# Hybrid decoder trunk: order of weighting, turning and scoring within a pair of attention heads

## What is computed

```
sc  = einsum('bqgrd,bgnd->bgrqn', qb, k_cmp)
o_c = einsum('bgrqn,bgnd->bqgrd', masked_softmax(sc, ...), v_cmp)
o_s = einsum('bgrqkl,bgqkld->bqgrd', masked_softmax(ss, m_s), vs)
o_w = einsum('bgrqk,bgkd->bqgrd', masked_softmax(sw, m_w), vw)
return gb[..., 0:1] * o_c + gb[..., 1:2] * o_s + gb[..., 2:3] * o_w
```

## Time and profile before

| what | value |
|---|---|
| median of 3 runs | 939.73 us (939.57 to 939.92) |
| the profiled execution's own time | 938.7 us |
| its span | 936.9 us |
| TensorE busy | 893.0 us, 95% |
| VectorE busy | 588.0 us, 63% |
| ScalarE busy | 523.8 us, 56% |
| the attention loop, rounds 1 to 7 | from about 636 to 686 us of the span |
| chain that ended last | TensorE 74%, ScalarE 12%, VectorE 10% |

### The profile page before, as it was taken

One profiled execution on the slowest core, in us unless ns is written; L12 is line 12 of the kernel. 1 busy time (PEld: TensorE's weight loads), 2 busy tenths in 40 slices (PEclk: granted clock), 3 DMA queues, 4 the chain that ended last, 5 costly groups with the idle time before them and its releaser, 6 DMA issues.

```text
span 936.9 us, 14028 instructions
## 1 busy us (share of the span) xinstructions
PE 893.0 (95%) x5289; PEld 758.1 (81%) x5289; DVE 588.0 (63%) x980; ACT 523.8 (56%) x931; POOL 23.9 (3%) x46
## 2 busy tenths in 40 slices
PE   6989999999999999999999999998889999999998
PEld 5989988787888878888888789886567888888876
DVE  5876985767666475555544676777757555554465
ACT  6645666767776474444543559356856544443352
POOL 6000000000000000000000000000000000000000
PEclk9999999999999999999999999999999999999999
DMA  9941211111114557777555555420034565654652
GB/s 342 337 139 43 91 46 46 46 46 46 46 54 171 186 161 247 236 226 224 187 189 176 195 178 177 136 91 1 2 115 154 184 188 186 191 193 158 195 185 93
DMA packets 105898, 138.28 MB, mean 148 GB/s; under 512 B 4585, under 2 KB 76786, under 8 KB 105842
## 3 DMA queue, kind: packets, MB, share of 16 engines
q1 hardware_dynamic: 103650, 130.15, 43.1%
q0 software_dynamic: 2160, 7.36, 2.0%
q10 hardware_dynamic: 32, 0.01, 0.0%
HBM read 136.45 MB, written 1.05 MB: 147 GB/s over the span
## 4 chain that ended last, share of the span: by engine, by line
PE 74%; ACT 12%; DVE 10%; issue 3%; DMA 1%; SPq 0%; ACTq 0%; DVEq 0%
PE ps L504 16%; PE ps L506 16%; PE ps L505 16%; PE ps L483 5%; DVE w_lo L1588 4%; ACT w_hi L1114 4%; PE ps L488 3%; PE ps L490 3%; PE ps L489 3%; PE ps L735 2%; DVE gdn L1655 2%; PE ps L715 2%; PE ps L1000 1%; ACT qkvT L1522 1%; ACT scr L1363 1%
## 5 line engine op out<-in xcount | busy, mean ns | idle before, releaser
L1588 DVE TENSOR_TENSOR w_lo<-w_raw,w_hi 128x2048 fp32r<-128x2048 f32 (+2 forms) x100 | 220.7, 2207 | 195.8 <-ACT w_hi L1114 195.7
L1114 ACT ACTIVATE w_hi<-w_raw 128x2048 fp32r<-128x2048 f32 (+2 forms) x100 | 184.5, 1845 | 181.8 <-PE ps L506 143.2
L504 PE MATMUL ps<-w_hi,x_hi 128*128 128x512 f32 x480 | 193.1, 402 | 5.3 <-DVE x_lo L1621 1.9
L506 PE MATMUL ps<-w_hi,x_lo 128*128 128x512 f32 x480 | 187.6, 391 | 0.0
L505 PE MATMUL ps<-w_lo,x_hi 128*128 128x512 f32 x480 | 187.2, 390 | 0.0
L504 PEld LDWEIGHTS ps<-w_hi,x_hi 128*128 128x128 f32 x480 | 90.2, 188 | 25.9 <-issue 4.5
L506 PEld LDWEIGHTS ps<-w_hi,x_lo 128*128 128x128 f32 x480 | 90.1, 188 | 19.5
L505 PEld LDWEIGHTS ps<-w_lo,x_hi 128*128 128x128 f32 x480 | 90.4, 188 | 16.7
L488 PE MATMUL ps<-x_hi,w_hi 128*128 128x256 f32 x320 | 91.4, 286 | 1.1 <-DVE w_lo L1588 0.8
L489 PE MATMUL ps<-x_lo,w_hi 128*128 128x256 f32 x320 | 90.6, 283 | 0.0
L490 PE MATMUL ps<-x_hi,w_lo 128*128 128x256 f32 x320 | 90.6, 283 | 0.0
(11 more groups left out here) (311 smaller groups left out, 1453.4 us busy)
## 6 DMA issues: line engine op xcount, KB each, us to landing
w_raw<-in_ffn_w_in SPq DMA_DIRECT2D x88, 512.0 KB, 4.6
w_raw<-in_ffn_w_out SPq DMA_DIRECT2D x40, 512.0 KB, 4.1
w_raw<-in_gdn_w_in SPq DMA_DIRECT2D x28, 512.0 KB, 4.7
gdn<-in_gdn_w_in SPq DMA_DIRECT2D x20, 512.0 KB, 7.6
w_raw<-in_gdn_w_out SPq DMA_DIRECT2D x16, 512.0 KB, 4.3
w_raw<-in_ple_w_gate SPq DMA_DIRECT2D x16, 512.0 KB, 4.6
w_raw<-in_kv_w SPq DMA_DIRECT2D x12, 512.0 KB, 4.3
qkvT<-in_cmp_w POOLq DMA_DIRECT2D x8, 512.0 KB, 4.9
```

The lines of the kernel that those rows point to most:

```text
L504: mm(o, hi, w_h, start=first and kk == 0, stop=False, skip_group_check=True)
L506: return mm(o, lo, w_h, start=False, stop=end and kk == n - 1, skip_group_check=True)
L1114: A(whi[:, place(stage, q), c0:c0 + n], ring_raw(u) if stage == "qkv" else raw[:, q, 0:n], ACT.Copy).then_inc(S["hi_done"], 1)
L1588: V.tensor_tensor(wlo[:, s, c0:c0 + n], ring_raw(u) if stage == "qkv" else raw[:, q, 0:n], whi[:, s, c0:c0 + n], ALU.subtract).then_inc(S[ ...
```

## The change

TensorE does the turns of both heads of a pair one behind the other, and the second scores of the next pair behind both. VectorE does the weights of both heads one behind the other, and all four maxima of the next pair behind both. ScalarE's order is untouched.

```diff
@@ TensorE, round p @@
                     scores(p + 1, 0)
                 turned(p, 0)
+                turned(p, 1)
                 if p < 7:
                     scores(p + 1, 1)
-                turned(p, 1)
                 if p == 1:
                     pe.wait_ge(S["q_sb"], 4)
                     cmp_scores(1, 1)
@@ VectorE, round p @@
                 weights(p, 0)
+                weights(p, 1)
                 if p < 7:
                     maxima(p + 1, 0, 0)
                     maxima(p + 1, 1, 0)
-                weights(p, 1)
-                if p < 7:
                     maxima(p + 1, 0, 1)
                     maxima(p + 1, 1, 1)
                 if p == 1:
```

## The result

The changed kernel takes 940.88 us (median of 20 runs, 939.72 to 943.18) against 939.83 us (20 runs, 938.25 to 940.65), a ratio of 1.0015 (95% interval 1.0008 to 1.0021). It is 1.05 us slower by the medians, 1.4 by the ratio. Measured again beside the experiments it was 941.97 us against 938.96, ratio 1.0027 (1.0016 to 1.0039). The prediction was 940.8, no difference beyond 0.2%.

What follows compares the result with a forecast made beforehand. No engine is full; a loop of handovers bounds the stage. Terms 0.55 - 0.02 + 0.55 - 0.07 + 0.06 = +1.07 us on the profiled 938.7 give 939.8, 940.8 on the median's scale; range 939.5 to 942.6.

Steps and rivals of the forecast that it cites:

- The 0.69 of idling goes, and the wait for the maxima takes its place: Ordinary rounds: TensorE's 0.69 idling before the output product is replaced by ScalarE's wait for second maxima; 6.79 against 6.82 us.
- The ordinary round: Rounds 2, 4, 5 and 6: 6.79 us each; -0.02 for round 2, about -0.07 for 4 to 6 together.
- (c): Condition for head 1's turns: the bank of head 0's first turn must be copied; latest of three, at 4.53 us.
- Round 1: Head 1's turns wait for weights, delaying second and compressed scores: +0.55 us taken, from values +0.45 and +0.62.
- The upper of my two values: Round 1 with turns taking 0.93 us: +0.62 us, against +0.45 if the turns need only 0.76.
- The sum: All rounds' terms added: 0.55 - 0.02 + 0.55 - 0.07 + 0.06 = +1.07 us.
- Round 3: Second compressed weights stand behind second maxima, delaying pair 3's weights: +0.55 us taken, from +0.44 (turns in 0.76) and +0.61.
- Round 7: No scores there; head 1's weights follow head 0's and start at 3.40 to 3.42 instead of 3.36: +0.06 us.
- Idling that simply goes: Next exponentials follow ScalarE's copies without waiting for second maxima: 0.75 us a round faster, 937.0 us; chance 0.07.
- VectorE's ring at more than its rows: VectorE's instructions in a round don't overlap: 7.11 us (942.1) or 7.83 us (944.9) where 6.79 was forecast; chance 0.13.
- Absorption behind the loop: The wait for the copy costs less, or something behind the stage takes up the loss: 939.7 to 940.0 us; chance 0.10.
- The granted clock should stay at 1.00: TensorE's clock in the profile after: 1.00, as before with TensorE idle for over a fifth of the first stretch.

Runs made afterwards that it cites:

- short_first: The changed kernel with ScalarE doing the short exponentials of both heads first, then the long ones of both; 942.84 us (ratio 1.0035).
- tail_in_gap: The changed kernel with VectorE's low half and weight quarter moved ahead of the second maxima, from round 3 on; 941.55 us (ratio 1.0021).
- after_heads: The changed kernel with the second scores made head by head, all of head 0 then all of head 1; 942.93 us (ratio 1.0036).
- before_heads: The kernel before, with the second scores made head by head; 943.55 us (ratio 1.0042).
- scale_in_gap: The changed kernel with four of five VectorE steps of the second compressed weights moved ahead of round 2's second maxima; 940.65 us (ratio 1.0016).
- short_first_before: The kernel before, with only ScalarE's exponentials reordered: short ones of both heads first, then long ones; 942.47 us (ratio 1.0035).
- dve_only: The kernel before with only VectorE's order changed: weights of both heads, then all maxima; 939.69 us (ratio 1.0001).
- round3_new: The kernel before, with the new order in round 3 alone, on both engines; 938.83 us (ratio 0.9996).
- pe_only: The kernel before with only TensorE's order changed: turns of both heads, then second scores; 944.31 us (ratio 1.0052).
- round1_old: The changed kernel, with round 1 alone in the order of before on both engines; 941.07 us (ratio 1.0018).
- short_first_gap: The changed kernel with short exponentials first, VectorE's low half, quarter and four compressed steps ahead of second maxima, round 1 in old order; 938.25 us (0.9993).

## Why the prediction was right, point by point

- **"The 0.69 of idling goes, and the wait for the maxima takes its place"**: right, and this is the mechanism. L1527 waits 0.68 to 0.73 in rounds 2, 4, 5 and 6, released by L2111. `short_first`, which fills just this wait, and `tail_in_gap`, which leaves it, tell it apart, and `after_heads`, where only the end of the second scores moved, leaves an ordinary round as it is.
- **The ordinary round** was mis-sized by up to 0.07: 6.85 or 6.86 in rounds 2, 5 and 6, and 6.79 in round 4, for 6.79. In round 6 of the change, from 677.12: turns of head 1 at 4.61, where (c) gave 4.53; second scores at 5.44 (5.34); maxima at 6.83 (6.72); long exponentials at 7.55 (7.47). The largest miss is the handover from the copy: the first copy starts at 681.09, lasts 0.49, and TensorE starts at 681.73, 0.15 behind its end, where I took the 0.06 of the output product. For the four rounds: +0.11 where I had -0.09.
- **Round 1** was +0.71 where I took +0.55. The upper of my two values, 0.62, was right for the turns (0.94 with the weights just in time, 641.41 to 642.35), and the output product came 0.10 later behind the compressed scores (643.63 to 645.53) than before (1.80). TensorE's weight loads show where this lies: from the first load to the output product it is 1.91 before and 1.90 after. Before, the first load stands 0.11 ahead of the first product (640.69 and 640.80), behind the transposes; after, behind the masks, both start at 643.63. `before_heads` and `after_heads`, with the same two orders, have 1.80 and 1.90 again. The sum had taken 1.80 over unchanged.

```profile
640.69 1.86 PEld L977 LDWEIGHTS ps<-cmp_keys,scr 128*128 128x128 f32 x16
...
643.63 1.86 PEld L977 LDWEIGHTS ps<-cmp_keys,scr 128*128 128x128 f32 x16 [0.21 <-issue]
```

- **Round 3** was +0.65 where I took +0.55, and here too the turns took 0.94 and not 0.76; the upper value, 0.61, is short by 0.04. `scale_in_gap` shows that VectorE's queue, not the turns, is the cause: with four steps out of the way round 3 falls below that of the kernel before.
- **Round 7**: +0.06, as predicted (head 1's weights at 687.41, 3.43 into the round, against 3.36).
- **The sum**: +1.07 predicted, +1.53 in the profile of the loop (0.16 of the difference from round 1, 0.10 from round 3, 0.20 from the ordinary rounds), +1.05 to +1.4 in the first 20 runs, ratio 1.0027 in the second measurement. The size of the median's shift was met more closely than that of the loop, which is luck within the scatter; the second median, 941.97, lies 1.2 above the forecast, still inside the range.
- **The rivals.** Idling that simply goes: refuted. VectorE's ring at more than its rows: refuted in `short_first`, where VectorE has no gap between second maxima and head 1's weights and keeps each start-to-start distance. By this the Trainium skill's section "The DRAIN you can't avoid" ("VectorE: DVE Perf Modes") again finds no support as a rule for adding up: in the changed kernel too, two maxima of 0.69 fill 1.29. The same section also says that an operation that is not held starts earlier, and with that the overlap agrees; the prediction had quoted only the first half. Absorption behind the loop: not seen. The span behind the table load lay between 242.8 and 243.4 in all profiles but one, long loop or short (in that one, `short_first_before`, the clock fell there). The two profiles of the change have 242.8 and 242.9 where before has 243.4, but `dve_only` and `round3_new`, with loops no longer than before, have 243.1 and 242.9; `pe_only`, with a loop 11 us longer, has 243.4. The shorter ends go with the long wait for `ple_w_in`, not with the loop; a few tenths either way can't be told.
- **"The granted clock should stay at 1.00"** held in the profiled executions of the change, but not for all its runs. This was the part that I had judged by a single profile of the kernel before, and it is the one with the most weight in the tail of the times.

## What to carry to other kernels

A wait that is visible on one engine is worth taking away only if the next thing on its ring is not held by what the reordering delays: here, in round 6, head 1's copies came 0.8 earlier in a round (5.25 against 6.06) and ScalarE still could not start, for the scores it needed had moved back by 1.3. Before swapping two steps, write down for every engine's list what then stands behind the later one; the two largest losses here (rounds 1 and 3) were not in the loop's regular body but in the rounds with extra work queued behind the moved step. And where two rings are equally long, an experiment that shortens one shows nothing until the other is shortened too.

## What the runs showed of the hardware

- **TensorE's clock in a loop of small waits.** In `round1_old` and `short_first` the granted clock fell to 0.50, the lower of its two levels, for about 3.5 us, behind single waits of at most 1.42 us between products. In `pe_only` it fell twice: behind waits of 0.42 and 0.98 it stood at 0.50 from about 641 to 650, and behind waits of 0.70 and 0.98 from about 665 to 668; that execution took 949.71 us. The loop of the kernel before has waits of up to 1.08, and its profile shows no fall. The changed kernel has in round 7 the very waits that `round1_old` has there, 1.29 and 0.33, ahead of the same products, and its profiles stay at 1.00. So no single wait tells it, and one pattern of waits goes with a fall in one execution and not in another. A mean clock of 0.998 or less stands in 1 of 5 runs of `pe_only`, 3 of 11 of `scale_in_gap`, 6 of 11 of `round1_old`, 2 of 11 of `tail_in_gap`, 4 of 6 of `short_first`, 2 of 5 of `short_first_before` and 5 of 28 of the change; in none of the 71 of the kernel before, nor of the 43 of `dve_only`, `after_heads`, `before_heads`, `round3_new` and `short_first_gap`. What makes the difference was not separated here. The Trainium skill, "TensorE: Matmul & The Clock Gate", section "Part 1: The HAM clock gate (the "warmup" mystery)", gives the same two levels, 1.2 and 2.4 GHz.
- **Products on the two halves of the rows take less time when they alternate.** Second scores: 1.28 alternating, 1.82 head by head, the same instructions.
- **The handover from ScalarE to TensorE took 0.06 or 0.15**, for the same copy instruction: 0.06 behind the second of two copies, ahead of the output product; 0.15 behind the first, ahead of the turns. What makes the difference was not tried.
